# First attention of a two-block transformer kernel: another order of its 32 groups, and the modulation block ahead of the scores

## The chip, the cores and the metric

The kernel runs on one core of a Trainium2 chip. The metric is the time of one execution on the device in microseconds, the median of several. All matrix products are in float32.

## The reference

Two blocks are computed one after the other on 256 latent and 256 context tokens of width 1024. The first has two layers (one with window and differential attention, one with latent attention), the second a recurrent mixer and a mixture of 16 experts. What the change touches is the attention of the first layer and the modulation vectors that are computed beside it:

```python
mx = (sc_x @ ada_w[l] + ada_b[l]).reshape(bsz, 6, 1, d)      # modulation, D -> 6 D, for each layer

def window_gqa_latent(q, k, v, k_ctx, v_ctx, sink):          # 8 "a" heads: windowed keys, a sink in the softmax
    ...
    s_loc = jnp.where(valid, s_loc, NEG_INF)
    p_loc, p_ctx, _ = joint_softmax(s_loc, s_ctx, s_sink)
    ...

def diff_attend(q, kv_parts, lam):                           # 4 "b" heads: (softmax1 - lam*softmax2) @ v
    ...
    outs = [jnp.einsum('bhqk,bkhd->bqhd', (p[:, 0] - lam * p[:, 1]).astype(v.dtype), v)
            for p, (_, v) in zip(probs, kv_parts)]

def diff_out(o, subln_g, lam_init):                          # after each b head: RMSNorm over its 128 values
    b, t = o.shape[:2]
    return (rmsnorm(o, subln_g) * (1.0 - lam_init)).reshape(b, t, -1)
```

## The kernel before

TensorE (PE), VectorE (DVE), ScalarE (ACT) and the DMA queue of SyncE each run a program written out by hand; semaphores tie them together. Weights stream through a ring of six slots (`ring`, 2 MB each); a slot is loaded again when `weights_used` tells that PE has read it. PSUM has eight banks: `take` hands out seven of them in rotation, so that each taking waits until the reader of the seventh last one is through, and bank 7 (`fixed`) holds the modulation sums.

The first attention is `attn0`, an object of class `Attention` with the 32 groups of `ab_groups`. A group is 128 queries of either one b head (two score maps, one difference of probabilities, values of width 128) or of two a heads (two maps, two sets of probabilities). It has 512 keys where `qc` is 0 or 1 ("long" from here on) and 256 where it is 2 or 3 ("short"). The list `ab_groups` holds 16 b groups (four heads by four `qc`: long, long, short, short, and so on) and then 16 a groups in the same pattern.

For group i the engines do this:

- PE (`pe`): `pe_turn(i)` transposes the probabilities when `probs_ready` allows (line 799), `pe_values(i - 1)`, `pe_scores(i + 3)`, then `pe_beside`.
- DVE (`dve`): `dve_probs(i)` (lines 877 to 886) scales the exponentials, `dve_stats(i + 2)` takes the maxima of the scores (lines 833 to 841; a long a group adds the window mask first, line 833), `dve_out(i - 2)` copies an output to H (line 892), then `dve_beside`.
- ACT (`act`): copies the transposed probabilities of i out of PSUM (line 864), then the exponentials of i + 2 (line 852), then `act_beside`.

Beside the attention the kernel computes the modulation of the next two layers. `turns(i)` deals 48 steps n to the 32 groups, one to an even group and two to an odd one. At each odd n PE runs `pe_ada_job`, which multiplies one 2 MB slot of `ada_w` (order row `ps<-ring,SC`): 24 jobs, none in the groups 0, 4, 8, ... and one in each other group. Four jobs fill bank 7. Then DVE copies it to `ADA` (`dve_ada_rows`, line 533), PE transposes that (`pe_ada_turn`, line 528), and DVE copies the result to `MOD` (`dve_ada_turned`, line 540). The first job of the next four writes bank 7 again, so it waits for `dve_ada_rows`. `pe_subln`, `act_subln` and `dve_subln` are the RMSNorm after each b head, a fixed number of groups behind its last group (`step_of`): a sum on PE, squares and a root on ACT, one scaling on DVE (line 1305).

Behind the attention PE goes on with the output projection (`pe_ab_out`); it waits for the last copies and for nothing else of this stage.

Of the kernel before, what the change touches and what calls it, by code (L numbers as in the profile page):

```python
# [36 lines left out]
BH, BV = 4, 128  # L37
# [112 lines left out]
def build(nc, A, tab_f, tab_m, vrows, out):  # L150
    es = ExitStack()
    with es:
# [26 lines left out]
        def ft(name, n=None, p=P):  # L179
            o, w = FT[name]  # L180
            return FTAB[0:p, o:o + (n or w)]
# [7 lines left out]
        def ar(off, *dims):  # L189
            n = int(np.prod(dims))  # L190
            a = AR[:, off:off + n]
            if len(dims) == 1:
                return a
            names = "abc"[:len(dims)]
            return a.rearrange(f"p ({' '.join(names)}) -> p {' '.join(names)}", **dict(zip(names, dims)))
# [60 lines left out]
        slot_of, after, last_in = [], [], [s - SLOTS for s in range(SLOTS)]  # L256
# [78 lines left out]
        for i in range(11):  # L335
            c = [512, 1024, 0, 1536, 2048, 2560, 3072, 3584, 4096, 4608, 5120][i]
# [5 lines left out]
        for e in range(NE):  # L342
            for i in range(8):
                w = A[("expert_w_gate_2", "expert_w_up_2")[i // 4]][0, e]
                part = w[(i % 4) * 256:(i % 4 + 1) * 256, :]
                if ("gu", e, i) in SPARE_OF:
                    n = SPARE_OF["gu", e, i]
# [176 lines left out]
        def pe_ada_turn(pe, l, g):  # L524
            b = take(pe, ("adaT", l, g))
            freed(pe, ("ada", l, g))
            for i in range(4):
                m = nc.tensor.transpose(ps[:, b, i * P:(i + 1) * P], ADA[:, g, i * P:(i + 1) * P], ident)  # L528
            m.then_inc(bank_full[b], 1)

        def dve_ada_rows(c, l, g):
            b = full_of(c.eng, ("ada", l, g))
            c.free(V.tensor_copy(ADA[:, g, :], ps[:, b, :]), ("ada", l, g))
# [38 lines left out]
            return range(3 * i // 2, 3 * (i + 1) // 2)  # L572

        def pe_ada_beside(pe, i):
            n, G = i // 2, (i - 9) // 8
            if i % 8 == 1 and 0 <= G < 6:
                pe_ada_turn(pe, 1 + G // 3, G % 3)
            if i % 2 and n < 24:
                pe_ada_job(pe, 1 + n // 12, n % 12)

        def dve_ada_beside(c, i):
            G = (i - 8) // 8
            if i % 8 == 0 and 0 <= G < 6:
                dve_ada_rows(c, 1 + G // 3, G % 3)
            G = (i - 10) // 8
            if i % 8 == 2 and 0 <= G < 6:
                dve_ada_turned(c, 1 + G // 3, G % 3)


# [188 lines left out]
        class Attention:  # L778
# [34 lines left out]
            def pe(self, pe):  # L813
                n = len(self.groups)
                for i in range(min(3, n)):
                    self.pe_scores(pe, i)
                for i in range(n):
                    self.pe_turn(pe, i)
                    if i:
                        self.pe_values(pe, i - 1)  # L820
                    if i + 3 < n:
                        self.pe_scores(pe, i + 3)
                    if self.pe_beside:
                        self.pe_beside(pe, i)
                self.pe_values(pe, n - 1)

            def dve_stats(self, c, i):
# [66 lines left out]
            def dve(self, c):  # L894
                n = len(self.groups)
                for i in range(min(2, n)):
                    self.dve_stats(c, i)
                for i in range(n):
                    self.dve_probs(c, i)
                    if i + 2 < n:  # L900
                        self.dve_stats(c, i + 2)
                    if i >= 2:
                        self.dve_out(c, i - 2)
                    if self.dve_beside:
                        self.dve_beside(c, i)
                for i in range(max(n - 2, 0), n):
                    self.dve_out(c, i)

# [345 lines left out]
        ab_groups = []  # L1254
# [7 lines left out]
        for h in range(0, AH, 2):  # L1262
            for qc in range(4):
                k0 = 0 if qc < 2 else TX
                maps = [(QK[64 * a:64 * a + 64, h // 2, qc * P:(qc + 1) * P], QK[64 * a:64 * a + 64, 4 + h // 4, k0:T2])
                        for a in range(2)]
                g = h // 4
                vals = [VA[:, t, g * 64:(g + 1) * 64] for t in range(k0 // P, 4)]
                mask = ft("window")[:, qc * TX:(qc + 1) * TX] if qc < 2 else None
                ab_groups.append(Group(("a", h, qc), maps, T2 - k0, DH ** -0.5, [vals, vals], 64,  # L1270
                                       H[:, h // 2, qc * P:(qc + 1) * P], mask, SINK[:, h:h + 2]))
        AB_TURNED = ar(14336, 2, 2, TX), ar(11264, 2, 2, TX)


# [5 lines left out]

        def step_of(i, after):

            h, r = divmod(i - after, 4)
            return h if r == 0 and 0 <= h < BH else None

        def pe_subln(pe, i):
            h = step_of(i, 7)
            if h is not None:
                pe_sums(pe, ("sub", h), 1, lambda k: sub_sq_at(h), T2,
                        lambda e, k: e.wait_ge(squares_ready.sem, sub_sq + h + 1))  # L1290

        def act_subln(c, i):
            h = step_of(i, 6)
            if h is not None:
                freed(c.eng, ("o", ("b", h, 3)))
                act_squares(c, sub_sq + h, 1, lambda k: H[:, 4 + h, :], lambda k: sub_sq_at(h), lambda e, k: None)
            h = step_of(i, 8)
            if h is not None:
                act_rstd(c, ("sub", h), sub_rs + h, BV, T2, sub_rs_at(h))

        def dve_subln(c, i):
            h = step_of(i, 9)
            if h is not None:
                c.eng.wait_ge(rstd_ready.sem, sub_rs + h + 1)
                c.mark(V.scalar_tensor_tensor(out=H[:, 4 + h, :], in0=H[:, 4 + h, :], scalar=LAM[:, 4:5],
                                              in1=sub_rs_at(h), op0=ALU.mult, op1=ALU.mult), o_ready, sub_o + h + 1)
# [955 lines left out]
        sub_sq, sub_rs, sub_o = squares_ready.plan(4), rstd_ready.plan(4), o_ready.plan(4)  # L2262
        attn0 = Attention(ab_groups, lambda i, u: AB_TURNED[i % 2][:, u, :, :], pe_ab_beside, act_subln, dve_ab_beside)
        y_at = [ar(0, KD, T2), ar(4096, KD, T2)]
# [42 lines left out]
        @block.tensor  # L2307
        def _(pe):
            pe_vectors(pe)
            pe_load(pe, "x0", lambda t, k: XIN[:, t, k * P:(k + 1) * P], 4, lambda e, t: e.wait_ge(x_loaded, 32))  # L2310
            pre0a.pe(pe)
            pe_adaln0(pe)
            pe_ab_in(pe, pre0a)
            pe.wait_ge(roped.sem, rope_base + len(ROPED))
            for t in range(4):
                freed(pe, ("v", 4, t))
            attn0.pe(pe)
            for i in range(48, 51):
                pe_ada_beside(pe, i)
            for qc in range(4):  # L2320
                freed(pe, ("o", ("a", AH - 2, qc)))
            pe.wait_ge(o_ready.sem, sub_o + 4)
            pe_ab_out(pe)
            pe_ffn0(pe)
            pe_mla_in(pe)
            pe.wait_ge(roped.sem, qrope + 4)
            for i in range(CH // 2):
                freed(pe, ("qn", i))
                freed(pe, ("km", i))
            for t in range(4):  # L2330
                for g in range(2):
                    freed(pe, ("vm", t, g))
            attn1.pe(pe)
            for qc in range(2):
                freed(pe, ("o", ("m", CH - 2, qc)))
            pe_mla_out(pe)
            pe_ffn1(pe)
            pe_hgrn_in(pe)
            pe_hgrn_state(pe)
            pe_hgrn_scores(pe)  # L2340
            pe_gates(pe)
            pre2f.pe(pe)
            pe_route(pe, pre2f)
            pe_experts(pe)
# [75 lines left out]
        @block.vector  # L2420
        def _(dve):
            c = Chain(dve, dve_step)
            dve.wait_ge(small_loaded, SMALL)
            dve_vectors(c)
            dve_load(c, "x0", 0, T2)
            dve_small(c)
            dve_adaln0(c)
            pre0a.dve(c)
            dve_lam(c)
            dve_ab_in(c)  # L2430
            attn0.dve(c)
            for i in range(48, 51):
                dve_ada_beside(c, i)
            for l in (1, 2):
                dve_mods(c, l)
            dve_ab_out(c)
            dve_ffn0(c)
            dve_mla_in(c)
            attn1.dve(c)
            dve_mla_out(c)  # L2440
            dve_ffn1(c)
            dve_hgrn_in(c)
            dve_hgrn_state(c)
            dve_hgrn_scores(c)
            dve_gates(c)
            pre2f.dve(c)
            dve_route(c)
            dve_experts(c)
            dve_final(c)
# [27 lines left out]
```

## Time and profile before

| | us |
|---|---|
| median of 3 runs | 2514.73 |
| the runs | 2508.41, 2514.92, 2514.73 |
| the profiled execution | 2511.16 |
| its span, first to last instruction | 2508.7 |
| PE busy in the span | 2052.7 (82%) |
| DVE busy | 760.0 (30%) |
| ACT busy | 443.6 (18%) |
| TensorE clock granted, mean | 0.907 |

The share of busy time is a mean over stages with different limits, so rows are read by stretch. In the timeline a row gives the start and the length of a run of equal instructions, and in brackets how long the engine stood idle before it and what ended that. Matmuls overlap a little in the record, so the cost of a step on PE is the distance from its start to the start of the next. An instruction count (x16) on PE counts two for each float32 matmul. The granted clock is 1.00 at 2.4 GHz and 0.50 at 1.2 GHz.

### The profile page before, as it was taken

To read this page: it belongs to the slowest core of one execution; us is meant where nothing else is said; L and a number is where in the kernel's file an instruction comes from. 1 tells how busy PE (TensorE), PEld (TensorE's weight loads), DVE (VectorE), ACT (ScalarE), POOL (GpSimd) and SP (SyncE) were. 2 spreads that over 40 slices of the span, in tenths; PEclk is the share of its full clock that TensorE was granted. 3 is DMA by queue.
4 is the path that set the end of the run, shared out by engine and by line. 5 is a ranking of instruction groups with operands and counts; after the bars stand their busy time and mean duration, and the time that the engine had idled before them with its cause. 6 is when DMAs were issued, how large, how long until landed. Compare 5 with 4: busy or idle time off the path is not lost.

```text
span 2508.7 us, 28673 instructions
## 1 busy us (share of the span) xinstructions
PE 2052.7 (82%) x11775; PEld 1284.3 (51%) x11775; DVE 760.0 (30%) x1667; ACT 443.6 (18%) x959; POOL 7.0 (0%) x15
## 2 busy tenths in 40 slices
PE   6998899999999999999999998865655566556555
PEld 3544368888747857899877776511111111111111
DVE  3117745555401556685036523100000000001001
ACT  3004534010101446311132221100000000000000
POOL 0000000000000000000000000000000000000000
PEclk9999999999999999999999989977788777787878
DMA  9557771321321531444622326799999999999997
GB/s 380 201 202 282 300 257 34 101 95 52 81 84 39 152 118 35 134 148 116 216 102 84 125 77 234 285 428 428 427 428 428 427 428 427 428 428 428 427 428 309
DMA packets 180737, 614.95 MB, mean 245 GB/s; under 512 B 26144, under 2 KB 121632, under 8 KB 146688
## 3 DMA queue, kind: packets, MB, share of 16 engines
q1 hardware_dynamic: 179792, 610.38, 62.4%
q0 software_dynamic: 816, 2.76, 0.4%
q8 instruction: 93, 1.52, 0.3%
q14 instruction: 36, 0.29, 0.0%
HBM read 612.06 MB, written 1.05 MB: 244 GB/s over the span
## 4 chain that ended last, share of the span: by engine, by line
PE 60%; DMA 34%; DVE 4%; ACT 1%; issue 1%; SPq 0%; DVEq 0%; ACTq 0%
PE ps L378 58%; DMA ring<-in_expert_w_up 12%; DMA ring<-in_expert_w_gate 10%; DMA ring<-in_expert_w_down 10%; DMA ring<-in_ab_w_in 1%; PE ps L799 1%; DVE ST L834 0%; DVE X L746 0%; DVE AR L745 0%; ACT AR L852 0%; ACT AR L864 0%; DVE H L697 0%; DVE AR L886 0%; PE ps L528 0%; DVE ps L833 0%
## 5 line engine op out<-in xcount | busy, mean ns | idle before, releaser
L378 PE MATMUL ps<-ring,AR 128*32 128x256 f32 (+2 forms) x4336 | 578.6, 634 | 348.5 <-DMA ring<-in_expert_w_gate 126.4
L378 PEld LDWEIGHTS ps<-ring,AR 128*32 128x32 f32 (+1 forms) x4336 | 196.3, 136 | 707.0 <-issue 243.8
L378 PE MATMUL ps<-H,ring 128*128 128x256 f32 (+2 forms) x2240 | 513.1, 387 | 7.6 <-ACT H L683 5.1
L378 PEld LDWEIGHTS ps<-H,ring 128*128 128x128 f32 x2240 | 403.1, 191 | 104.1 <-issue 55.7
L378 PE MATMUL ps<-AR,ring 128*128 128x256 f32 (+2 forms) x1548 | 358.8, 390 | 3.9 <-DVE AR L989 2.9
L378 PEld LDWEIGHTS ps<-AR,ring 128*128 128x128 f32 x1548 | 273.4, 191 | 84.4 <-issue 53.1
L378 PE MATMUL ps<-AR 128*128 128x128 f32 (+6 forms) x1200 | 175.0, 340 | 19.7 <-ACT AR L852 8.6
L2216 DVE TENSOR_TENSOR AR<-AR,ps 128x512 f32<-128x512 f32 x16 | 11.0, 687 | 576.3 <-PE ps L378 576.3
L378 PEld LDWEIGHTS ps<-AR 128*128 128x128 f32 (+3 forms) x1200 | 128.7, 184 | 48.8 <-issue 40.2
L2227 DVE TENSOR_TENSOR AR<-ps,X 32x256 f32<-32x256 f32 x64 | 26.9, 420 | 282.1 <-PE ps L378 280.4
L2202 ACT ACTIVATE AR<-ps 128x512 f32<-128x512 f32 x16 | 9.6, 597 | 528.5 <-PE ps L378 528.4
L378 PE MATMUL ps<-ring,H 128*128 128x512 f32 (+1 forms) x224 | 76.6, 502 | 0.0
L378 PE MATMUL ps<-ring,SC 128*32 128x512 f32 x576 | 71.3, 622 | 2.7 <-DMA ring<-in_ada_w 2.7
L740 DVE TENSOR_TENSOR H<-H 128x256 f32<-128x256 f32 x21 | 8.9, 425 | 200.9 <-ACT H L726 200.8
L378 PE MATMUL ps<-ring 128*128 128x256 f32 x288 | 68.0, 379 | 0.0
L2208 ACT ACTIVATE AR<-ps 128x512 f32<-128x512 f32 x16 | 9.6, 597 | 321.8 <-PE ps L2182 321.8
L834 DVE TENSOR_REDUCE ST<-ps 128x1 f32<-128x512 f32 (+1 forms) x96 | 57.8, 602 | 26.5 <-PE ps L378 24.4
L378 PE MATMUL ps<-H,AR 128*128 128x128 f32 (+3 forms) x328 | 61.7, 340 | 2.4 <-ACT H L644 2.4
L852 ACT ACTIVATE AR<-ps,ST 128x512 f32<-128x512 f32 (+1 forms) x96 | 59.2, 616 | 24.2 <-DVE ST L841 21.1
L378 PEld LDWEIGHTS ps<-ring 128*128 128x128 f32 x288 | 54.7, 190 | 7.4
L378 PEld LDWEIGHTS ps<-ring,H 128*128 128x128 f32 x224 | 37.5, 191 | 37.8 <-issue 37.7
L378 PEld LDWEIGHTS ps<-H,AR 128*128 128x128 f32 (+2 forms) x328 | 48.8, 186 | 10.3 <-issue 4.5
(284 smaller groups left out, 1408.4 us busy)
## 6 DMA issues: line engine op xcount, KB each, us to landing
ring<-in_expert_w_gate SPq DMA_DIRECT2D x64, 2048.0 KB, 23.3
ring<-in_expert_w_down SPq DMA_DIRECT2D x64, 2048.0 KB, 23.1
ring<-in_expert_w_up SPq DMA_DIRECT2D x61, 2048.0 KB, 23.3
ring<-in_ada_w SPq DMA_DIRECT2D x36, 2048.0 KB, 10.6
ring<-in_ffn_w SPq DMA_DIRECT2D x44, 1024.0 KB, 7.6
ring<-in_w_in SPq DMA_DIRECT2D x12, 2048.0 KB, 7.9
ring<-in_ffn_w SPq DMA_DIRECT2D x16, 1408.0 KB, 7.1
ring<-in_ab_w_in SPq DMA_DIRECT2D x4, 2048.0 KB, 16.0
```

Source lines behind the costliest of these rows:

```text
L378: m = nc.tensor.matmul(out_, lhsT=lhsT, rhs=rhs, start=start, stop=stop)
L740: ins = V.tensor_tensor(self.SQ(0)[:, self.t], self.SQ(0)[:, self.t], self.SQ(k)[:, self.t], ALU.add)
L799: m = nc.tensor.transpose(ps[:, b, j * P:(j + 1) * P], PR[:, i % 2, u, j * P:(j + 1) * P], ident)
L834: c.step(V.reduce_max(st[:, m:m + 1], ps[:, b, 0:g.nk], axis=AX_X))
L852: c.free(S.activation(PR[:, i % 2, m, 0:g.nk], ps[:, b, 0:g.nk], ACT.Exp, bias=st[:, 2 + m:3 + m], scale=g.scale, accum_out=st[:, 6 + m:7 ...
L2202: c.free(S.activation(GT, ps[:, b, :], ACT.Silu), ("hg", e))
L2208: c.free(S.activation(HT.rearrange("p a b -> p (a b)"), ps[:, b, :], ACT.Copy), ("ht", e))
L2216: c.free(V.tensor_tensor(HS, GT, ps[:, b, :], ALU.mult), ("hu", e))
L2227: ins = V.tensor_tensor(YE[32 * q:32 * q + 32, g, t * TX:(t + 1) * TX], ps[32 * t:32 * t + 32, b, 0:TX], GFR[32 * t:32 * t + 32, t, :], AL ...
```

## The change

Three things are changed, all in and around `attn0`.

1. The list of groups is dealt anew: two b groups, then one a group, eight times over; the last eight a groups (heads 4 to 7) stay at the end. The groups at places 0 to 11 are then b long, b long, a long, b short, b short, a long, b long, b long, a short, b short, b short, a short, and places 12 to 23 repeat this. The steps of `pe_subln`, `act_subln` and `dve_subln` follow the new places of each head's last b group (4, 10, 16, 22) with smaller distances (4; 3 and 5; 6).
2. On PE `pe_beside` stands ahead of `pe_scores(i + 3)`; on DVE `dve_beside` stands ahead of `dve_out(i - 2)`.
3. In the modulation block the copy of bank 7 moves from step n = 8, 16, ... to 9, 17, ..., the transpose from 9, ... to 11, ..., and the copy of that from 10, ... to 12, .... The loop behind the attention ends at 52 instead of 50.

```diff
         def pe_ada_beside(pe, i):
-            n, G = i // 2, (i - 9) // 8
-            if i % 8 == 1 and 0 <= G < 6:
+            n, G = i // 2, (i - 11) // 8
+            if i % 8 == 3 and 0 <= G < 6:
                 pe_ada_turn(pe, 1 + G // 3, G % 3)
...
         def dve_ada_beside(c, i):
-            G = (i - 8) // 8
-            if i % 8 == 0 and 0 <= G < 6:
+            G = (i - 9) // 8
+            if i % 8 == 1 and 0 <= G < 6:
                 dve_ada_rows(c, 1 + G // 3, G % 3)
-            G = (i - 10) // 8
-            if i % 8 == 2 and 0 <= G < 6:
+            G = (i - 12) // 8
+            if i % 8 == 4 and 0 <= G < 6:
                 dve_ada_turned(c, 1 + G // 3, G % 3)
...
                         self.pe_values(pe, i - 1)
+                    if self.pe_beside:
+                        self.pe_beside(pe, i)
                     if i + 3 < n:
                         self.pe_scores(pe, i + 3)
-                    if self.pe_beside:
-                        self.pe_beside(pe, i)
...
                         self.dve_stats(c, i + 2)
+                    if self.dve_beside:
+                        self.dve_beside(c, i)
                     if i >= 2:
                         self.dve_out(c, i - 2)
-                    if self.dve_beside:
-                        self.dve_beside(c, i)
...
+        ab_groups = [ab_groups[n] for i in range(8) for n in (2 * i, 2 * i + 1, 16 + i)] + ab_groups[24:]
+        head_end = [[g.key for g in ab_groups].index(("b", h, 3)) for h in range(BH)]
...
         def step_of(i, after):
 
-            h, r = divmod(i - after, 4)
-            return h if r == 0 and 0 <= h < BH else None
+            return head_end.index(i - after) if i - after in head_end else None
 
         def pe_subln(pe, i):
-            h = step_of(i, 7)
+            h = step_of(i, 4)
...
         def act_subln(c, i):
-            h = step_of(i, 6)
+            h = step_of(i, 3)
...
-            h = step_of(i, 8)
+            h = step_of(i, 5)
...
         def dve_subln(c, i):
-            h = step_of(i, 9)
+            h = step_of(i, 6)
...
-            for i in range(48, 51):
+            for i in range(48, 53):
                 pe_ada_beside(pe, i)
```

Two places show how the instructions move. The first is PE at groups 21 and 22. In the rows, `L799` is a turn, `ps<-AR 64x128` or `128x128` the value products, `128x256` or `128x512` the scores of the group three further, `ps<-ring,SC` a modulation job and `L528` the modulation transpose. Before:

```order
L799 MATMUL ps<-FTAB,AR 128x128 x8
L378 MATMUL ps<-AR 64x128 x8
L378 MATMUL ps<-AR 128x512 x2
L378 MATMUL ps<-ring,SC 32x512 x8
L799 MATMUL ps<-FTAB,AR 128x128 x4
L378 MATMUL ps<-AR 64x128 x8
L378 MATMUL ps<-AR 128x512 x2
L528 MATMUL ps<-FTAB,AR 128x128 x4
L378 MATMUL ps<-ring,SC 32x512 x8
L799 MATMUL ps<-FTAB,AR 128x128 x4
```

After, for the groups at the same places:

```order
L799 MATMUL ps<-FTAB,AR 128x128 x2
L378 MATMUL ps<-AR 64x128 x4
L378 MATMUL ps<-ring,SC 32x512 x8
L378 MATMUL ps<-AR 128x512 x2
L799 MATMUL ps<-FTAB,AR 128x128 x2
L378 MATMUL ps<-AR 128x128 x2
L378 MATMUL ps<-ring,SC 32x512 x8
L378 MATMUL ps<-AR 128x512 x2
L799 MATMUL ps<-FTAB,AR 128x128 x4
```

The job now stands between the value products and the scores, so the scores are the last thing ahead of the next turn, and the modulation transpose has left this group.

The second place is DVE where it copies bank 7 for the fourth time (`L533`): group 21 before, group 22 after. `L836` to `L839` end the maxima of an a group, `L892` is the output copy, `L1305` (`L1306` after) the scaling of a b head, `L877` begins the probabilities of the next a group. Before:

```order
L836 SCALAR_TENSOR_TENSOR ST<-ST,SINK 128x2
L838 TENSOR_TENSOR ST<-SINK,ST 128x2
L839 TENSOR_SCALAR ST<-ST 128x2
L892 COPY H<-ps 128x128
L1305 SCALAR_TENSOR_TENSOR H<-H,LAM,AR 128x512
L533 COPY AR<-ps 128x512
L877 TENSOR_TENSOR ST<-ST 128x2
L878 RECIPROCAL ST<-ST 128x2
L882 TENSOR_SCALAR AR<-AR,ST 128x256 x2
```

After:

```order
L833 TENSOR_TENSOR ps<-ps,FTAB 128x256
L834 TENSOR_REDUCE ST<-ps 128x1
L833 TENSOR_TENSOR ps<-ps,FTAB 128x256
L834 TENSOR_REDUCE ST<-ps 128x1
L836 SCALAR_TENSOR_TENSOR ST<-ST,SINK 128x2
L838 TENSOR_TENSOR ST<-SINK,ST 128x2
L839 TENSOR_SCALAR ST<-ST 128x2
L1306 SCALAR_TENSOR_TENSOR H<-H,LAM,AR 128x512
L533 COPY AR<-ps 128x512
L892 COPY H<-ps 128x128
```

The copy of bank 7 has moved ahead of the output copy, and into the group whose job on PE writes that bank again.

## Rows read from the trace of the kernel before

**Rows 1.** Busy time by stretch: stretch, length, five engines, TensorE clock, DMA share, GB/s.

```profile
190.00:349.00 159.00, 134.99 (x988) 65.80 (x987) 112.56 (x327) 78.23 (x205) 0.00 (x0) 0.95 0.81 306
349.00:1700.00 1351.00, 1276.68 (x6601) 1001.87 (x6599) 558.23 (x1155) 317.41 (x667) 5.08 (x8) 0.97 0.39 132
```

**Rows 2.** Timeline of PE: start, length, line, what, count; steps without a wait.

```profile
208.18 2.12 PE L378 MATMUL ps<-AR 128*128 128x128 f32 x12
210.22 1.92 PE L378 MATMUL ps<-ring,SC 128*32 128x512 f32 x16
212.08 0.44 PE L799 MATMUL ps<-FTAB,AR 128*128 128x128 f32 x2
212.36 1.24 PE L378 MATMUL ps<-AR 128*128 128x128 f32 x8
...
245.77 1.12 PE L378 MATMUL ps<-AR,FTAB 128*128 128x512 f32 x2
246.73 0.60 PE L528 MATMUL ps<-FTAB,AR 128*128 128x128 f32 x4
247.26 1.92 PE L378 MATMUL ps<-ring,SC 128*32 128x512 f32 x16
...
289.63 1.09 PE L799 MATMUL ps<-FTAB,AR 128*128 128x128 f32 x8
290.65 0.66 PE L378 MATMUL ps<-AR 128*64 128x128 f32 x8
```

**Rows 3.** Timeline of PE: the first turn, four waits, and the end of the stage.

```profile
199.16 1.08 PE L799 MATMUL ps<-FTAB,AR 128*128 128x128 f32 x4 [4.03 <-DVE AR L886]
...
224.08 0.41 PE L799 MATMUL ps<-FTAB,AR 128*128 128x128 f32 x2 [2.28 <-DVE AR L886]
...
279.71 1.43 PE L378 MATMUL ps<-AR 64*128 64x512 f32 x4 [2.24 <-ACT AR L852]
281.07 3.26 PE L378 MATMUL ps<-ring,SC 128*32 128x512 f32 x16
...
292.61 0.70 PE L378 MATMUL ps<-AR 64*128 64x256 f32 x4 [1.30 <-ACT AR L852]
...
300.19 0.80 PE L799 MATMUL ps<-FTAB,AR 128*128 128x128 f32 x4 [1.76 <-DVE AR L882]
...
348.15 1.03 PE L378 MATMUL ps<-H,ring 128*128 128x256 f32 x4
```

**Rows 4.** DVE groups by shape, 192 to 349: busy us, mean ns, idle before.

```profile
L834 DVE TENSOR_REDUCE ST<-ps 128x1 f32<-128x512 f32 x32 | 22.1, 691 | 4.5 <-PE ps L378 3.5
L834 DVE TENSOR_REDUCE ST<-ps 128x1 f32<-128x256 f32 x32 | 13.6, 424 | 12.5 <-PE ps L378 11.7
L892 DVE COPY H<-ps 128x128 f32<-128x128 f32 x32 | 9.3, 292 | 6.9 <-PE ps L378 5.9
L882 DVE TENSOR_SCALAR AR<-AR,ST 128x512 f32<-128x512 f32 x16 | 7.8, 487 | 0.6
L833 DVE TENSOR_TENSOR ps<-ps,FTAB 128x256 f32<-128x256 f32 x16 | 6.9, 432 | 3.9 <-PE ps L378 3.5
L886 DVE SCALAR_TENSOR_TENSOR AR<-AR,ST 128x512 f32<-128x512 f32 x8 | 6.0, 751 | 0.3
L882 DVE TENSOR_SCALAR AR<-AR,ST 128x256 f32<-128x256 f32 x16 | 5.7, 354 | 0.6
L878 DVE RECIPROCAL ST<-ST 128x2 f32<-128x2 f32 x32 | 5.3, 166 | 1.3 <-ACT AR L852 0.2
L533 DVE COPY AR<-ps 128x512 f32<-128x512 f32 x6 | 4.1, 691 | 6.0 <-PE ps L378 5.9
L886 DVE SCALAR_TENSOR_TENSOR AR<-AR,ST 128x256 f32<-128x256 f32 x8 | 3.9, 484 | 0.3
```

**Rows 5.** Busy time by stretch, columns as in rows 1: two at the lower clock.

```profile
200.00:202.00 2.00, 1.42 (x7) 0.55 (x5) 1.83 (x6) 1.59 (x5) 0.00 (x0) 0.50 0.00 0
282.00:284.00 2.00, 2.00 (x16) 0.32 (x8) 1.83 (x6) 0.00 (x0) 0.00 (x0) 0.55 0.74 311
```

More of the change, by code:

```diff
@@ L2431, in _ @@
             attn0.dve(c)
-            for i in range(48, 51):
+            for i in range(48, 53):
                 dve_ada_beside(c, i)
```

## Prediction, made before the changed kernel had run

> **What bounds the kernel now.** First the busy time by stretch. The change acts between 192 and 348 us only; in that stage PE is busy for 135.0 of 159 us and DVE for 112.6, so PE bounds it with 24 us of idle time, and DVE is close behind. In the 1351 us that follow PE is busy for 1276.7, at a weight stream of 132 GB/s, so it is PE that is waited for there, and what the stage gains or loses passes on one for one until the experts [rows 1]. The experts stream weights, but each load waits for a slot that PE has read, so they start later or earlier by the same amount. DMA is at 0.81 inside the stage and PE never stands waiting for a weight slot in the waits that I read there.
>
> Then the timeline of PE inside the stage. From the first turn at 199.16 to the first product of the output projection at 348.15 it is **149.0 us** [rows 3]. The waits there are of three kinds: a turn that waits for DVE's probabilities (2.28 at 224.08, because DVE first waited for a modulation job and copied bank 7; 1.76 at 300.19, the same), scores that wait for a bank which ACT's exponentials still hold (2.24 at 279.71, 1.30 at 292.61), and the start [rows 3]. Besides the waits there is the lower clock. It was granted around 200 and around 282 [rows 5]; the job at 281.07 takes 3.26 us there where one at full clock takes 1.92 [rows 3, 2].
>
> **Prices on PE**, as distances between starts [rows 2]: a job 212.08 - 210.22 = 1.86; long value products and long scores together 2.04, so 1.02 each; the short pair 1.24 less the overlap of 0.07, so 0.58 each; a sum 0.96; a modulation transpose 0.53; a turn of a long a group 1.02, of a short b group 0.28, hence 0.57 for a short a group and 0.5 for a long b group (four transposes, as in the modulation transpose). Jobs, groups, sums and transposes of the stage add up to 24 x 1.86 + 16 x 2.04 + 16 x 1.16 + 8 x (0.5 + 0.28 + 1.02 + 0.57) + 4 x 0.96 + 6 x 0.53 = 121.8, of which the first three scores (3.1) stand ahead of the first turn. So PE has 118.8 us of work in the 149.0.
>
> **Prices on DVE** [rows 4], with 0.03 of gap behind each instruction and 0.17 for each small one (the reciprocal's size). Maxima: b long 2 x 0.691 + one small = 1.65, b short 1.12; a short 2 x 0.424 + three small = 1.51; a long adds two masks of 0.432 to the long maxima: 2.98. Probabilities: b long two small + 0.487 + 0.751 = 1.70, b short 1.28, a long two small + 2 x 0.487 = 1.42, a short 1.16. Output copy 0.32, copy of bank 7 0.72, scaling of a b head 0.78 (the 512-wide form of line 886), copy to MOD 0.22. Eight groups of each of the four kinds, with four scalings and six copies of either kind, make about 121 us of work on DVE, whatever the order.
>
> **What the new order does.** Part by part:
>
> The *dealing* puts long masked a groups (DVE 2.98 + 1.42 + 0.32 = 4.7, PE 3.1 and a job in three of four) between b groups (DVE 3.7 or 2.7). Nothing is added or removed.
>
> The *block ahead of the scores* takes away the waits for banks: with a job of 1.86 between values and scores, a bank that was late by 1.30 or 1.76 is free. At groups 0, 4, 8, ... there is no job, but there the waits below are the longer ones. But it also ties PE and DVE more closely. Before, DVE had the scores of i + 2 while PE still did a job; now the scores are the last work ahead of turn i, and DVE can begin maxima i + 2 only when both this is done and probabilities i are. Then it does maxima i + 2, the block, an output copy and probabilities i + 1, and that is what turn i + 1 waits for. So each group costs the longer of two sums: PE's (turn i, values i - 1, block, scores i + 3), or DVE's (maxima i + 2, block, copy, probabilities i + 1), the latter with 0.17 + 0.10 for the two signals where PE was the late one. Nothing is carried over from one group to the next.
>
> The *later copy of bank 7* removes the two waits of 2.28 and 1.76. In its place stands a new wait: copy n = 9 is now in the group of the job that writes bank 7 again, on DVE behind the maxima, on PE behind the value products. Queued behind that job are the scores, and behind these DVE's next maxima. It strikes at groups 6, 11, 17, 22 and 27. At 22 it is worst: maxima of group 24 (a long) 2.98, scaling 0.78, copy 0.72, signal 0.17 = 4.65, then 0.10 + job 1.86 + scores 1.02 = 7.63, where PE alone would have 3.74.
>
> The sum over the groups (P: PE's sum decides; D: DVE's; B: the wait for bank 7):
>
> 0 D 4.68, 1 P 3.96, 2 P 4.92, 3 D 4.85, 4 D 3.39, 5 P 4.04, 6 B 4.94, 7 P 4.49, 8 D 3.21, 9 P 3.74, 10 D 4.18, 11 B 5.35 (51.8 so far); 12 D 5.27, 13 P 4.49, 14 P 5.88, 15 D 4.85, 16 D 4.17, 17 B 4.91, 18 P 4.49, 19 P 3.96, 20 P 3.13, 21 P 3.74, 22 B 7.63, 23 D 4.99 (109.3); 24 D 3.47, 25 P 4.92, 26 P 5.43, 27 B 6.41, 28 D 4.30, 29 P 4.43, 30 P 3.45, and 31 with the end (turn, values twice, job, copies of DVE, transpose) 5.4.
>
> For example group 3: 0.17 + maxima of group 5 (a long) 2.98 + 0.32 + probabilities of group 4 (b short) 1.28 + 0.10 = 4.85, against PE's 0.28 + 1.02 + 1.86 + 1.02 = 4.18. Together **147.1 us at full clock**, 28 us of it idle on PE.
>
> **The lower clock.** Comparing like with like needs its price before. At the start the two turns and values up to 206 cost about 1.7 more than at full clock in time that nothing else hides; the stretch at 280 costs 1.34 on the job and 0.4 on the scores [rows 3, 2], 1.7; a third one, which I read in the timeline behind the wait of 1.76 at 300.19, about 2.0. Together 5.4, an estimate from these rows. So the old order at full clock would be 143.6 and the new one 147.1. What the clock will do in the new order no row shows. Bounds: the start alone, 1.7, or that and four more stretches of up to 2.5, 11.7. I take 5.4 as before, since there are waits of PE of 3 to 4 us at groups 0, 12 and 22 in the new order, and before it fell once behind 4.03, once behind 2.24 and not behind the 2.28 at 224.08. That gives 152.5 against 149.0: **3.5 us slower**.
>
> The profiled execution took 2511.16, so its own time becomes 2514.7. It lies 3.6 below the median shown; the mean of the four times shown is 2512.3. I put the 3.5 on that mean: 2515.8, rounded to 2516.
>
> **Rivals.**
>
> *Slower than can be missed.* The waits at groups 12 (3.6 idle), 22 (3.8), 27 (2.8) and 28 (2.1) each bring the lower clock, and a job and scores then run at half speed behind them, inside the chain that DVE waits for. Speaks for it: two of the three such stretches before came behind waits of 2.3 or less [rows 3]. Speaks against: 2.28 at 224.08 brought none. Four stretches of 2.5 with the start's 1.7 give 147.1 + 11.7 = 158.8, 9.8 slower, 2522. It decides where the lower clock costs more than 9.4 in the stage.
> The Trainium skill, "TensorE: Matmul & The Clock Gate", section "HAM oscillation", tells the same of loops whose bursts of matmuls are parted by waits: they pay for a cold clock again and again. That rule speaks against this change.
>
> *Faster.* DVE and PE share the stage more evenly, because long masked groups no longer follow each other, and the tie that I describe is looser than I think (DVE begins maxima with the first of two score maps). Then PE has its work of 118.8, the start's extra 3.6, the end's 1.3, a wait of 2.3 in each eight groups and 1.7 of low clock: 134.6, 14.4 faster, 2498. For it: the a groups took most of the waits before [rows 3]. Against it: the sum above gives DVE or bank 7 the last word in 16 of 32 groups.
> This is what the Trainium skill, "Perfetto Trace Analysis", section "Optimization Strategy", advises: where the most-contended engine changes over time, interleave the regimes. Here both regimes have PE ahead of DVE by little, so the trace leaves it small room.
>
> *It does not reach the end.* A slip of some us is taken up by the expert stream, and the time is that of before, 2512. Against it: PE paces all that lies between [rows 1].
>
> **How the numbers follow.** 0.57 for the forecast (its own range 2509 to 2521), 0.28 for the slower rival, 0.11 for the faster one, 0.04 for the last. The faster rival lies outside the range, the slower one inside: 2506 to 2524. 0.3% is 7.5 us, about what a measurement of this kernel can tell from no change. Faster by more 0.11, within 0.61 (forecast and the last), slower by more 0.28.
>
> **What the profile of the changed kernel would show.** The distance from first turn to first product of the output projection tells the sum: 152 if right. Group 0 takes 4.7 instead of 2.8. The waits of scores for exponentials are gone almost everywhere. New waits of modulation jobs for the copy of bank 7 stand at groups 6, 11, 17, 22 and 27, together about 10 us, the longest near 3.9. DVE has less idle time behind scores for short groups and never runs ahead of PE by more than a group. I am wrong if turns wait less than 10 us in all, if the job at group 22 waits less than 3, or if the lower clock fills over 20 us of the stage.

## The result and the profile of the changed kernel

The changed kernel takes 2515.76 us (median of 12 runs, 2513.79 to 2520.28), the kernel before 2511.87 (12 runs, 2508.41 to 2514.92). The ratio is 1.0016, 95% interval [1.0009, 1.0024]: **3.9 us slower**, a difference of 0.16% that is clear of the noise and inside the forecast's range. The profiled execution took 2515.66, its span is 2513.1, against 2511.16 and 2508.7.

Between the two profiles most of it arises in the stage. First the busy time of the stage (columns as in rows 1), which answers to the first row of [rows 1]:

```profile
190.00:352.00 162.00, 132.56 (x988) 64.27 (x987) 112.94 (x329) 78.13 (x205) 0.00 (x0) 0.95 0.80 302
```

PE has the same 988 instructions as before, and DVE and ACT are busy as long as before within 0.4 us; PE's idle time has grown from 24.0 us (in the 159 us of rows 1) to 29.4 us (in 162). Then the timeline of PE, which answers to [rows 3]: first turn, four of the five jobs that wait for the copy of bank 7 (groups 11, 17, 22 and 27; that of group 6 is left out), the turn of group 13 with the job behind it, and the first product of the output projection.

```profile
198.21 0.63 PE L799 MATMUL ps<-FTAB,AR 128*128 128x128 f32 x4 [3.60 <-DVE AR L886]
...
248.29 1.92 PE L378 MATMUL ps<-ring,SC 128*32 128x512 f32 x16 [1.43 <-DVE AR L533]
...
256.49 0.63 PE L799 MATMUL ps<-FTAB,AR 128*128 128x128 f32 x4 [3.41 <-DVE AR L886]
...
259.17 2.76 PE L378 MATMUL ps<-ring,SC 128*32 128x512 f32 x16
...
279.65 1.92 PE L378 MATMUL ps<-ring,SC 128*32 128x512 f32 x16 [1.22 <-DVE AR L533]
...
302.35 3.35 PE L378 MATMUL ps<-ring,SC 128*32 128x512 f32 x16 [3.78 <-DVE AR L533]
...
329.42 3.47 PE L378 MATMUL ps<-ring,SC 128*32 128x512 f32 x16 [2.65 <-DVE AR L533]
...
350.71 4.50 PE L378 MATMUL ps<-H,ring 128*128 128x256 f32 x20
```

From 198.21 to 350.71 it is **152.5 us**, 3.5 more than before. Two of the jobs (302.35, 329.42) take 3.35 and 3.47 instead of 1.92: they stand behind the two longest waits for the copy, and the clock has fallen. The job at 259.17, behind the turn that waited 3.41, takes 2.76. What PE waited for in the stage, before and then after (engine, line, waited for, us, times, longest; the start's wait counts in both):

```profile
PE ps L378 <- ACT AR L852: 9.5, 8, 2.2
PE ps L799 <- DVE AR L886: 7.1, 4, 4.0
PE ps L378 <- DVE H L892: 2.8, 3, 1.3
PE ps L799 <- DVE AR L882: 1.8, 1, 1.8
```

```profile
PE ps L799 <- DVE AR L886: 10.9, 4, 3.6
PE ps L378 <- DVE AR L533: 9.7, 5, 3.8
PE ps L799 <- DVE AR L882: 2.4, 4, 1.0
PE ps L378 <- DVE H L892: 2.3, 4, 1.2
PE ps L378 <- ACT AR L852: 1.0, 1, 1.0
```

The waits of scores for exponentials (line 852) are gone but for one. In their place stand the five waits for the copy of bank 7 (line 533) and longer waits of turns for probabilities. The reason for the worst of them is to be seen on DVE in group 22:

```profile
297.84 0.43 DVE L833 TENSOR_TENSOR ps<-ps,FTAB 128x256 f32<-128x256 f32 x1 [0.76 <-PE ps L378]
298.31 0.69 DVE L834 TENSOR_REDUCE ST<-ps 128x1 f32<-128x512 f32 x1
...
300.82 0.75 DVE L1306 SCALAR_TENSOR_TENSOR H<-H,LAM,AR 128x512 f32<-128x512 f32 x1
301.60 0.69 DVE L533 COPY AR<-ps 128x512 f32<-128x512 f32 x1
...
306.86 0.43 DVE L833 TENSOR_TENSOR ps<-ps,FTAB 128x256 f32<-128x256 f32 x1 [3.07 <-PE ps L378]
```

The copy of 0.69 comes 3.8 us after the start of the maxima, the job on PE waits for it, the scores wait for the job, and DVE then stands idle for 3.07 until it has these scores. Both engines wait in turn.

### The profile page after: what moved, and what is told of

The parts are those of the page before. It is cut to its first block, busy times and chain, and to the rows that moved or that the text cites. A ratio compares the mean times of both kernels' runs of the same rounds, so it can differ in the third digit from the quotient of the medians.

```text
span 2513.1 us, 28673 instructions
## 1 busy us (share of the span) xinstructions
PE 2043.7 (81%) x11775; PEld 1283.0 (51%) x11775; DVE 760.0 (30%) x1667; ACT 443.1 (18%) x959; POOL 7.0 (0%) x15
## 3 DMA queue, kind: packets, MB, share of 16 engines
q0 software_dynamic: 816, 2.76, 0.4%
## 4 chain that ended last, share of the span: by engine, by line
PE 59%; DMA 34%; DVE 5%; issue 1%; ACT 1%; SPq 0%; DVEq 0%; ACTq 0%
PE ps L378 57%; DMA ring<-in_expert_w_up 12%; DMA ring<-in_expert_w_gate 11%; DMA ring<-in_expert_w_down 10%; DMA ring<-in_ab_w_in 1%; PE ps L799 1%; DVE ST L834 1%; DVE AR L745 0%; DVE X L746 0%; DVE H L697 0%; DVE ps L833 0%; DVE AR L882 0%; DVE AR L533 0%; PE ps L528 0%; SPq L2365 0%
## 5 line engine op out<-in xcount | busy, mean ns | idle before, releaser
L378 PE MATMUL ps<-ring,AR 128*32 128x256 f32 (+2 forms) x4336 | 572.4, 627 | 356.2 <-DMA ring<-in_expert_w_up 127.5
```

The costliest lines, as they stand in the source:

```text
L378: m = nc.tensor.matmul(out_, lhsT=lhsT, rhs=rhs, start=start, stop=stop)
```

## The experiments

Each was timed beside the kernel before on the same chip. "Stage" is the distance from first turn to first output product in its profile. "Low clock" is the time within 190 to 350 us that PE's clock stood at 1.2 GHz, from the granted clock of windows of 1 us.

| kernel | stage us | low clock us | time, median us | kernel before, median us | ratio, 95% interval |
|---|---|---|---|---|---|
| before | 149.0 | 17.1 | | | |
| changed | 152.5 | 17.1 | 2515.76 | 2511.87 | 1.0016 [1.0009, 1.0024] |
| deal_only | 148.6 | 17.0 | 2513.83 | 2509.88 | 1.0014 [1.0005, 1.0023] |
| ahead_only | 157.3 | 23.9 | 2521.64 | 2509.88 | 1.0040 [1.0028, 1.0053] |
| early_copy | 155.1 | 27.3 | 2518.66 | 2512.39 | 1.0024 [1.0013, 1.0035] |
| copy_first | 145.4 | 13.7 | 2509.86 | 2509.88 | 0.9997 [0.9988, 1.0006] |
| copy_first_behind | 151.8 | 23.9 | 2514.76 | 2509.88 | 1.0016 [1.0007, 1.0025] |
| kept_busy | 148.6 | 10.2 | 2509.49 | 2512.39 | 0.9992 [0.9983, 1.0001] |
| mixed_order | 133.2 | 3.4 | 2495.17 | 2512.39 | 0.9934 [0.9921, 0.9946] |
| mixed_order2 | 133.6 | 3.4 | 2497.25 | 2512.39 | 0.9942 [0.9928, 0.9955] |

### The new order of the groups alone (deal_only)

The changed kernel with the blocks and their steps put back:

```diff
-                    if self.pe_beside:
-                        self.pe_beside(pe, i)
                     if i + 3 < n:
                         self.pe_scores(pe, i + 3)
+                    if self.pe_beside:
+                        self.pe_beside(pe, i)
...
-            n, G = i // 2, (i - 11) // 8
-            if i % 8 == 3 and 0 <= G < 6:
+            n, G = i // 2, (i - 9) // 8
+            if i % 8 == 1 and 0 <= G < 6:
                 pe_ada_turn(pe, 1 + G // 3, G % 3)
```

> Only the new order of the groups (with the RMSNorm steps that follow it); the modulation block stays behind the scores and behind the output copy, and its steps stay at 8, 9 and 10. Read as the distance from the first turn to the first product of the output projection: 149.0 us in the kernel before, 152.5 in the changed one. Theory A, that the changed kernel is slower because the block ahead of the scores ties PE to DVE group by group and because the modulation job waits for the copy of bank 7: neither is here, so the stage is between 144 and 149 and the time 0 to 5 us below that of the kernel before. Theory B, that the dealing itself costs (long masked groups among the b groups): the stage is about 152 and the time some 3 to 4 us above. No job waits for line 533 in either.

The stage is 148.6, within 0.4 of the kernel before: **the dealing by itself is worth nothing in the stage** and does no harm there either. Theory B is refuted for the stage. Inside it the waits only change their kind: those of scores for exponentials (line 852) fall from 9.5 to 5.2 us, those of turns for probabilities (line 886) grow from 7.1 to 12.5. The time was expected 0 to 5 us below the kernel before and is 3.9 us (0.14%) above it, so that part of the expectation failed. In the profile the stage is not the reason: it ends at 347.60, 0.55 earlier than before, and the loss comes at the very end, which is told below.

### The other two parts on the old order (ahead_only)

The kernel before with the blocks ahead of scores and output copy and with the later steps.

> The old order of the groups with the other two parts: the modulation block ahead of the scores and of the output copy, and its steps at 9, 11 and 12. Theory A: by the same sum of the longer of PE's and DVE's work in each group, 147 us at full clock and some 5 for the lower clock, so a stage of about 152 and a time 3 to 4 us above that of the kernel before, with waits of jobs for line 533 at groups 6, 11, 17, 22 and 27 of 0.5 to 3 us. Theory B: the stage is that of before or shorter, 145 to 149, since the dealing is not here.

Theory A had the direction, and the size was too small: 157.3, where 152 was expected. Its waits on PE in the stage:

```profile
PE ps L799 <- DVE AR L886: 7.9, 6, 4.0
PE ps L378 <- ACT AR L620: 7.7, 3, 2.8
PE ps L378 <- DVE AR L533: 6.9, 5, 2.4
PE ps L378 <- DVE H L892: 3.9, 4, 2.5
```

The five waits for line 533 are about as expected (6.9 us, each 0.2 to 2.4). Those for line 620, 7.7 us, were in nobody's sum: ACT takes the root out of the bank of the RMSNorm sum, and scores wait for that bank. The root comes a group behind the sum, as in the kernel before, where scores waited for it 0.2 at most; here they wait 2.3 to 2.8 us at three places. A sum of PE and DVE alone does not hold where ACT holds a bank.

### New order and block ahead, with the old steps (early_copy)

```diff
-            G = (i - 9) // 8
-            if i % 8 == 1 and 0 <= G < 6:
+            G = (i - 8) // 8
+            if i % 8 == 0 and 0 <= G < 6:
                 dve_ada_rows(c, 1 + G // 3, G % 3)
```

> The changed kernel with the steps of the modulation block where they were (copy of bank 7 at 8, transpose at 9, copy to MOD at 10), so new dealing and block ahead of scores without the later steps. No job waits for the copy in another group's place, but DVE waits in groups 5 and 21 for the job of the same group before it can copy, and the turn behind waits for DVE. By the sums: groups 5 and 21 grow by 2.0 and 1.5, group 22 falls by 2.2, 6 by 0.5, 17 by 0.7: stage 151 to 154, about the changed kernel. If the later steps were the whole fault of the changed kernel, the stage would be that of the copy-first kernel, 145 to 147.

155.1, just above the 151 to 154 expected, and far from the 145 to 147 of the other case: so the later steps are no fault by themselves; without them the stage is 2.6 longer and the clock is low for 10 us more. Against deal_only (148.6), which has the same order and the same steps and differs in the place of the block alone, it is 6.5 longer: with the old steps the block ahead of the scores is a loss. One more wait than expected is in it: a modulation transpose in group 27 waits 2.98 for an output copy that stands on DVE behind the maxima and the copy of bank 7:

```profile
332.10 1.12 PE L528 MATMUL ps<-FTAB,AR 128*128 128x128 f32 x4 [2.98 <-DVE H L892]
333.14 3.64 PE L378 MATMUL ps<-ring,SC 128*32 128x512 f32 x16
```

### The copy of bank 7 ahead of the maxima (copy_first)

```diff
                     self.dve_probs(c, i)
+                    if self.dve_beside:
+                        for m in turns(i):
+                            dve_ada_copy(c, m)
                     if i + 2 < n:
                         self.dve_stats(c, i + 2)
```

> The changed kernel with the copy of bank 7 moved on DVE ahead of the maxima of the same group, so that no job of PE waits long for it. Theory A, sum of the groups: 6, 11, 17, 22 and 27 fall by 0.4, 0.9, 0.5, 1.4 and 0.7, together 4.0 us, and the stretches of lower clock behind the long waits of groups 22 and 27 (1.4 and 1.5 us) go too: stage 145.5 to 148.5, 4 to 7 us below the changed kernel, 0 to 3 below the kernel before. A rival, that DVE is the limit anyway and the copy only takes another place in its row: stage 152, same time as the changed kernel. The long waits for line 533 are gone in both.

The stage is 145.4, 7.1 less than the changed kernel (4.0 from the sums and 2.9 from the clock were expected, a stage of 145.5 to 148.5). Group 22 in its timelines, first DVE, then PE:

```profile
296.84 0.69 DVE L533 COPY AR<-ps 128x512 f32<-128x512 f32 x1
297.57 0.43 DVE L835 TENSOR_TENSOR ps<-ps,FTAB 128x256 f32<-128x256 f32 x1
```

```profile
297.41 0.44 PE L801 MATMUL ps<-FTAB,AR 128*128 128x128 f32 x2
297.69 0.61 PE L378 MATMUL ps<-AR 128*128 128x128 f32 x4
298.23 1.92 PE L378 MATMUL ps<-ring,SC 128*32 128x512 f32 x16
```

The copy is through before the job needs the bank, the job waits for nothing, and it runs at full clock: the group takes 5.15 instead of 9.01. Group 27 does less well than expected, 6.53 for 7.93: its wait for the copy is gone, but its scores now wait 2.80 for ACT's root, and the clock is low behind that wait too.

```profile
327.40 0.70 PE L378 MATMUL ps<-AR 64*128 64x256 f32 x4 [2.80 <-ACT AR L622]
```

So **the place of this one copy is what the stage of the changed kernel loses by**. The time is that of the kernel before, 2509.86 against 2509.88; of the 3.6 us that the stage is shorter than before nothing can be seen in the medians.

### The same with the block behind the scores (copy_first_behind)

```diff
-                    if self.pe_beside:
-                        self.pe_beside(pe, i)
                     if i + 3 < n:
                         self.pe_scores(pe, i + 3)
+                    if self.pe_beside:
+                        self.pe_beside(pe, i)
```

(and on DVE the block behind the output copy again).

> The new order of the groups, the later steps 9, 11 and 12 with the copy of bank 7 ahead of the maxima, but the modulation block behind the scores and behind the output copy as before. If the tie of PE and DVE by the block ahead of the scores costs more than the waits for banks that it covers, this is shorter than the one with the block ahead: stage 141 to 145, 4 to 8 us below the kernel before. If covering the bank waits is worth more, it is longer than that one: 147 to 150, with scores that wait for line 852 by 1.3 us at a dozen places.

151.8, 6.4 longer than with the block ahead. The first of the two expectations falls, the second was still too low. Three of its waits on PE in the stage, and one on DVE:

```profile
PE ps L801 <- DVE AR L888: 7.2, 4, 3.6
PE ps L378 <- DVE H L894: 7.1, 6, 2.5
PE ps L378 <- ACT AR L854: 6.5, 4, 3.9
DVE AR L533 <- PE ps L378: 8.0, 4, 3.1
```

Scores wait for banks again, 13.6 us for the second and third row together. But the last row is a second cost, and no expectation had it: with the job behind the scores, DVE's copy of bank 7 comes too early ahead of the maxima and waits for the job, 8.0 us in four waits, and the maxima stand behind it. In copy_first DVE has no such wait. So the 6.4 us are not the price of the bank waits alone, and the runs do not part the two. The block ahead of the scores gains on this order with the later steps and the early copy (copy_first), and loses with the old steps (early_copy against deal_only). On the old order, ahead_only, it came with a loss; there the late root and the late copy are in it, and were not parted from it.

### PE kept busy inside three waits (kept_busy)

The changed kernel; the value products ahead of the wait are repeated with the same result:

```diff
-                        self.pe_values(pe, i - 1)
+                        self.pe_values(pe, i - 1, {12: 4, 22: 5, 27: 3}.get(i, 0) if self.pe_beside else 0)
```

> The changed kernel, in which PE repeats the value products of the group before (same operands, same bank, same result) 4 times in group 12, 5 times in 22 and 3 times in 27, inside the waits of 3.4, 3.8 and 2.65 us that it has there. It adds 2.3, 2.7 and 1.7 us of work and no wait. If the waits bring the lower clock, the stretches at 257, 301 and 329 go and the stage falls by about 4.4, from 152.5 to 148, the time by 4. If the clock falls there for another reason, it still falls, and the stage stays at 152 to 153.

148.6: **more work, and 3.9 us less** than the changed kernel. The whole is level with the kernel before (0.9992, interval up to 1.0001). The same places as above, groups 12 to 13 and 22, in its timeline:

```profile
256.82 0.63 PE L799 MATMUL ps<-FTAB,AR 128*128 128x128 f32 x4 [1.67 <-DVE AR L886]
...
258.70 1.92 PE L378 MATMUL ps<-ring,SC 128*32 128x512 f32 x16
...
301.05 1.92 PE L378 MATMUL ps<-ring,SC 128*32 128x512 f32 x16 [1.55 <-DVE AR L533]
```

The jobs behind the waits take 1.92 again, where the changed kernel has 2.76 at 259.17 and 3.35 at 302.35; groups 13, 22 and 27 fall from 6.00, 9.01 and 7.93 to 4.37, 7.59 and 6.53, by 1.6, 1.4 and 1.4, and all others stay within 0.6 (group 1 grows by 0.5; the low clock of the start lasts longer in this run). The three stretches of low clock are gone. That the waits bring the low clock there is thereby shown, and its price as well: 1.4 to 1.6 us for each.

### Orders in which PE's and DVE's sums are alike (mixed_order, mixed_order2)

The copy-first kernel; the indices are places in the old list. The waits for the last group of a head follow the new places. mixed_order2 has another such list.

```diff
-        ab_groups = [ab_groups[n] for i in range(8) for n in (2 * i, 2 * i + 1, 16 + i)] + ab_groups[24:]
+        ab_groups = [ab_groups[n] for n in (2, 18, 3, 0, 1, 19, 6, 16, 4, 17, 5, 8, 7, 22, 10, 20,
+                                            9, 11, 12, 14, 13, 23, 15, 21, 26, 24, 27, 25, 28, 30, 31, 29)]
```

> The copy-first kernel with the 32 groups in an order chosen so that in each group DVE's sum (maxima of i + 2, probabilities of i + 1, copies) is about as long as PE's (turn i, values i - 1, block, scores i + 3): long a groups are met by PE work that is as long. If the tie group by group (the longer of the two sums decides) is what the stage costs, the sum falls by about 13 us against the copy-first kernel: first-turn-to-output distance of 132 to 136 us where the copy-first kernel has 145.4, and a time 9 to 15 us (0.4 to 0.6%) below the kernel before. If waits for banks or ACT are the limit instead, the order of the groups is worth 0 to 3 us and the distance stays above 142.

> The same with another such order, and the block on DVE behind the output copy as in the kernel before (PE's block stays ahead of the scores). By the same sum 0.5 us shorter than the other: distance 131 to 136, 9 to 15 us below the kernel before. Tells how much the result hangs on one lucky order or on where the clock falls.

Stages of 133.2 and 133.6, and the times are 0.66% and 0.58% below the kernel before: **both beat the kernel before and the changed one**: by 17.2 and 15.1 us the kernel before that ran beside them, where 9 to 15 were expected. Busy time of the stage, and what PE waits for in it, in mixed_order:

```profile
190.00:331.00 141.00, 128.46 (x989) 62.95 (x988) 113.07 (x329) 78.13 (x205) 0.00 (x0) 0.99 0.90 349
```

```profile
PE ps L801 <- DVE AR L888: 4.4, 5, 3.3
PE ps L378 <- DVE H L894: 1.8, 4, 0.8
PE ps L378 <- ACT AR L622: 1.5, 2, 0.8
PE ps L378 <- ACT AR L854: 1.5, 2, 0.9
```

DVE has the same 113 us of work as in all of them, now in 141 instead of 162. Of PE's waits 3.26 is the start. The clock has fallen only there. Two quite different orders give the same within 0.4 us, both inside the stage that the sums had given (132 to 136, 131 to 136), so it is the balance and not one lucky list. Not all of the 12.2 us below copy_first is the balance itself: the clock is low for 10.2 us less, three stretches of 3.4 us. At the 1.4 to 1.6 us that such a stretch cost in kept_busy's places that is 4 to 5 us, an estimate. The waits that brought the low clock went with the new order, so the two gains come together; no run parted them.

## Why the prediction was right, and where it was not

**The sum.** 147.1 at full clock and 5.4 for the low clock made 152.5, and 152.5 was measured. Group by group: 0 takes 4.68 (4.68 said), 2 4.83 (4.92), 3 4.89 (4.85), 6 4.72 (4.94), 7 4.40 (4.49), 11 5.59 (5.35), 12 5.29 (5.27), 14 5.69 (5.88), 17 5.30 (4.91), 26 5.58 (5.43). The rule, that each group costs the longer of PE's and DVE's sums, holds to 0.4 us in 24 of the 32; four of the others (1, 13, 22, 27) are those in which the low clock is. That the total came out to the decimal is luck: the clock cost some 0.6 more than the 5.4, and the sums were 0.5 too high.

Some terms were wrong and in part cancelled. Groups 4 and 16 take 2.89 and 2.85 for 3.39 and 4.17: the turn of a long a group begins when the first of its two sets of probabilities is ready, and I had counted both (0.5), and while turn 16 waited 1.09 for ACT, DVE had already begun the work of group 16. So it is not true that nothing is carried over from one group to the next. Group 15 takes 5.81 for 4.85: 1.09 of it is a turn that waits for ACT's root at 273.99, a wait that I had left out with all of ACT. My list of PE's waits in the kernel before was short by a kind as well: scores that wait for an output copy (line 892), 2.8 us in three waits.

**The waits for the copy of bank 7.** Said: five, about 10 us together, the longest near 3.9. Measured: 9.7, the longest 3.8. copy_first takes them away, and with them 7.1 us of the stage, twice what the changed kernel lost against the one before.

**The low clock.** I took 5.4, as before. In the changed kernel it is 1.6 at the start (group 1 takes 5.52 for 3.96) and, by kept_busy, 4.4 in the three stretches: 6.0. Three of the four places that the slower rival named (12, 22, 27) did bring it, each at 1.4 to 1.6 and not 2.5. So the mechanism of that rival is real, and its price was too high by more than a third; group 28, which waited only 1.23, did not bring it. The clock is not what sets the two kernels apart: it is low for 17.1 us in both, and costs 6.0 in the changed one for the 5.4 that I estimated before.

**The three signs of being wrong** did not come: turns waited 14.4 us (10.9, 2.4 and 1.1; the start's 3.6 is in them), the job at group 22 waited 3.78, and the clock was low for 17.1 us.

**From the stage to the whole.** I said one for one. In the profiles the whole is 4.4 longer, and it adds up in another way: 0.95 less, because the first turn comes earlier (PE is ahead by 1.0 us already at 75 us, before anything that was changed), 3.5 more in the stage, and 1.8 more behind it. Half of the 1.8 arises near 1030 us: there the kernel before has its clock at 1.2 GHz for 3.4 us and the changed one for 6.8 (granted clock 0.94 from 1031 to 1034 us, against 0.66 from 1033 to 1037, at about the same products), and the same products take 0.9 us more. copy_first loses its 3.6 like this: its first turn comes 0.7 later, and 2.5 us go behind the stage, 1.3 of them near 1030. Each profile is one execution, and why the clock stays low longer there was not tried.

So that 3.9 was measured where 3.5 was forecast is in part luck. In the other kernels the change of the median and the change of the stage against the kernel before lie up to 4.3 us apart: 3.9 against -0.4 in deal_only, 11.8 against 8.3 in ahead_only, 0.0 against -3.6 in copy_first, -2.9 against -0.4 in kept_busy. What is shown is the stage, 3.5 us longer, and its reason; that the 3.9 us of the median are these 3.5 is likely and not shown.

**The faster rival and its rule.** I gave the interleaving of regimes small room, because PE and DVE are near each other in both halves of the old order. That was wrong in its reason: on this order the dealing alone is worth 0.4 us, but with the copy in its place another dealing is worth 12, the clock included. What matters is not the share of the two engines over ten groups but their two sums in each single group. The Trainium skill's advice in "Perfetto Trace Analysis", section "Optimization Strategy", to interleave regimes with different most-contended engines, goes with what mixed_order shows (12.2 us below copy_first), but not with the order of this change (0.4 us).

**The slower rival's rule.** The Trainium skill, "TensorE: Matmul & The Clock Gate", section "HAM oscillation", tells of a low clock that is paid for again behind each of the waits between bursts of matmuls. kept_busy agrees at three places, 4.4 us in all. But it does not speak against this change in particular, as the kernel before pays nearly as much.

## What to carry to other kernels

In a loop in which two engines hand work to each other once per turn, write down for each turn both sums, from the last thing one gives the other to the next thing it gets back; in this kernel each turn cost about the longer one, so work that is saved on the shorter side is lost. Where a third engine holds a buffer, as ACT did in ahead_only and in group 27 of copy_first, add its waits. Order the turns so that the two sums match turn by turn, not on average. A small copy that frees a buffer belongs ahead of the long work of its engine when its data are ready by then and the job that waits for it stands ahead of the scores that this engine needs next; where its data came later (copy_first_behind), the same place made it wait.

## What the runs showed of the hardware

**Useless matmuls can shorten a kernel.** In kept_busy the value products in groups 12, 22 and 27 (in 12 with the scores behind them) take 3.04, 2.84 and 1.97 us for 1.29, 0.61 and 0.66 in the changed kernel: 5.3 us of matmuls more (6.7 were expected). They took 3.9 us off the stage, because the clock stayed at 2.4 GHz behind the waits.

**The end of the kernel has two lengths.** The last eight products (of the last expert) in the kernel before, and in deal_only:

```profile
2497.29 3.70 PE L378 MATMUL ps<-AR 128*128 128x512 f32 x8 [1.99 <-DVE AR L2227]
```

```profile
2498.06 5.40 PE L378 MATMUL ps<-AR 128*128 128x512 f32 x8 [2.00 <-DVE AR L2228]
```

The same instructions take 3.70 or 5.40, by the clock that stands there. From the issue of the last weight load to the end of the span it is 37.9 in the kernel before, in the changed one, in copy_first and in kept_busy, but 40.9 in deal_only and mixed_order2, 41.2 in early_copy, 41.3 in copy_first_behind, 41.6 in mixed_order and 41.8 in ahead_only. Beside the eight products the job before them is slower there, 3.23 instead of 1.93 in deal_only. That is where deal_only's profile, whose span is 2.5 us longer, loses its time. Each profile is one execution. Whether a kernel always meets the same clock at its end, or whether it is chance in each run (the runs of the kernel before range over 8 us), was not tried and stays open; so a difference of 3 us in the median of one kernel against another is not proof of anything in the part that was changed.
